# Router products in four column groups, more zero products in waits, and four reorderings of a two-block transformer kernel

## The reference

```
first_block:                                   # weights read once, 384 MB of them in the experts
  mod = silu(c) @ w_ada + b_ada                # six vectors: shifts, scales, gates
  h = rms_norm(x)*(1+sc1)+sh1 ; y = mixer(h)   # sliding attention + gated linear attention, @ w_out
  x = x + gt1*rms_norm(y, g_post_mix)
  h = rms_norm(x)*(1+sc2)+sh2
  logits = h @ w_router + b_router             # 256 x 32; the top 4 of 32 experts for each row
  y = sum over chosen e of gate_e * expert_e(h)   # expert: (u @ w1 + b1), limited swiglu, @ w2 + b2
  x = x + gt2*rms_norm(y, g_post_ffn)
second_block:
  h += 0.5*swiglu(rmsnorm(h), gate, up, down)              # 1024 -> 2816 -> 1024
  z = rmsnorm(h) @ w_in
  attn = moba_attention(q, k, v)                           # from z
  gm = u * (W_s @ layernorm(v) + b_s)                      # chunked spatial gating, from gelu(z)
  h += (sigmoid gates * (attn @ w_a, gm @ w_g)) @ w_out
  h += 0.5*swiglu(...) ; return rmsnorm(h, final_norm)
```

## Time and profile before

| what | us |
|---|---|
| median of 3 runs | 1649.52 |
| lowest, highest | 1648.58, 1654.21 |
| the profiled execution | 1654.21 |
| its span, first to last instruction | 1652.5 |
| PE busy in the span | 1459.1 (88%) |
| mean granted clock of TensorE | 0.94 of full |

### The profile page before, as it was taken

The page is one execution under the profiler, slowest core; times in us unless marked ns, Lnnn a source line. Parts: engine busy times, 40 slices in busy tenths (PEclk is TensorE's granted clock), DMA queues, the critical chain, the costliest instruction groups (busy, mean ns, idle before and its releaser), DMA issues.

```text
span 1652.5 us, 20611 instructions
## 1 busy us (share of the span) xinstructions
PE 1459.1 (88%) x8409; PEld 844.1 (51%) x8414; DVE 589.2 (36%) x957; ACT 471.5 (29%) x836; POOL 123.5 (7%) x254
## 2 busy tenths in 40 slices
PE   5999987896868787897687888899999999999998
PEld 3768433342322232332232333248888878788886
DVE  3675212220110111221110211146654677666654
ACT  3544201110110110111000101046553674565643
POOL 2001301110110110110110110000000010000000
PEclk9998999997888897999898998899999999999999
DMA  9998999999999999999999999976555433555440
GB/s 383 410 359 348 372 424 426 425 424 426 425 425 424 427 423 425 423 386 427 425 422 423 425 424 425 408 311 225 185 183 199 179 129 126 214 206 195 178 162 26
DMA packets 76953, 547.45 MB, mean 331 GB/s; under 512 B 8660, under 2 KB 9044, under 8 KB 11112
## 3 DMA queue, kind: packets, MB, share of 16 engines
q1 hardware_dynamic: 75744, 542.95, 80.6%
q10 hardware_dynamic: 1032, 2.16, 0.4%
HBM read 544.03 MB, written 1.06 MB: 330 GB/s over the span
## 4 chain that ended last, share of the span: by engine, by line
PE 65%; DMA 25%; issue 4%; DVE 3%; POOL 1%; ACT 1%; PEldq 1%; SPq 0%; POOLq 0%; DVEq 0%; ACTq 0%
PE bank L309 62%; DMA slot<-w_mlp 24%; PE bank L313 2%; DMA slot<-w_in_tail 1%; PEldq L85 1%; SPq L336 0%; DVE u_l L327 0%; DVE u_g L323 0%; DVE u_l L324 0%; DVE u_s L319 0%; PE bank L1451 0%; POOL oh L324 0%; POOL ow L324 0%; DVE h L327 0%; DVE XL L319 0%
## 5 line engine op out<-in xcount | busy, mean ns | idle before, releaser
L309 PE MATMUL bank<-slot,xt 128*32 128x512 f32 (+1 forms) x2048 | 377.7, 682 | 71.6 <-DMA slot<-w_mlp 70.7
L309 PEld LDWEIGHTS bank<-slot,xt 128*32 128x32 f32 (+1 forms) x2048 | 95.2, 129 | 345.6 <-issue 178.7
L309 PE MATMUL bank<-wht,XH 128*128 128x512 f32 x528 | 207.5, 397 | 4.4 <-DVE wlt L319 2.7
L327 DVE SCALAR_TENSOR_TENSOR wlt<-slot,colt,wht 128x512 fp32r<-128x512 f32 x248 | 177.3, 760 | 79.1 <-ACT wht L316 78.8
L323 DVE TENSOR_SCALAR u_g<-bank 64x512 f32<-64x512 f32 (+1 forms) x34 | 23.3, 686 | 510.8 <-PE bank L309 503.5
L309 PE MATMUL bank<-wht,XL 128*128 128x512 f32 x528 | 204.0, 391 | 0.0
L309 PE MATMUL bank<-wlt,XH 128*128 128x512 f32 x528 | 203.9, 391 | 0.0
L316 ACT ACTIVATE wht<-slot,colt 128x512 fp32r<-128x512 f32 x248 | 164.4, 718 | 92.3 <-PE bank L309 92.2
L316 ACT ACTIVATE u_s<-u_g 64x512 f32<-64x512 f32 (+1 forms) x34 | 21.4, 630 | 533.0 <-DVE u_g L323 533.0
L309 PE MATMUL bank<-slot,at 128*32 128x256 f32 (+1 forms) x1664 | 160.3, 431 | 6.8 <-DMA slot<-w_mlp 3.6
L309 PEld LDWEIGHTS bank<-slot,at 128*32 128x32 f32 (+1 forms) x1664 | 65.9, 116 | 95.6 <-issue 65.5
(11 more groups left out here) (321 smaller groups left out, 1485.5 us busy)
## 6 DMA issues: line engine op xcount, KB each, us to landing
slot<-w_mlp SPq DMA_DIRECT2D x384, 1024.0 KB, 27.0
slot<-gu SPq DMA_DIRECT2D x44, 1024.0 KB, 4.8
slot<-w_ada SPq DMA_DIRECT2D x24, 1024.0 KB, 10.0
slot<-down SPq DMA_DIRECT2D x22, 1024.0 KB, 4.8
slot<-w_in SPq DMA_DIRECT2D x18, 1024.0 KB, 5.3
slot<-w_out SPq DMA_DIRECT2D x8, 1024.0 KB, 8.4
slot<-w_gate SPq DMA_DIRECT2D x8, 1024.0 KB, 4.8
slot<-w_br_a SPq DMA_DIRECT2D x2, 1024.0 KB, 5.2
```

What stands on the lines that cost most here:

```text
L309: return pe(lambda e: e.matmul(o, l, r, start=start, stop=stop), *after, **kw)
L327: return dve(lambda e: e.scalar_tensor_tensor(o, a, s, b, op0, op1), *after)
```

## The change

- In the wait for the first weights (L620 to L627): 5 more zero products.
- residual gets later: with it, both gained products and the two sums in h are emitted by the returned function. Only the second half of the last residual ahead of the tail uses it.
- logits: four products side by side in the four column groups (weights wrt of 32 columns, 128 moving columns of h2t), two sets of four for each half; ScalarE copies the 128x128 sum to at, and one product with the new constant sum4 adds the four groups. The transposes of half 1 are emitted in two fours, with zero products between; rows_out moves behind the second logits_out on ScalarE's queue. From the router to the gather there are now 19 zero products instead of 7, on bank 6 instead of bank 4.
- swiglu: u_l goes ahead of the product u_s.
- layer_norm moves from the last span of w_in2 to the third span of gates, spatial_gate from the first span of gates to the fourth.
- first_merged splits one piece more before its transposes.

```diff
@@ -225,6 +225,7 @@
         stat0, stat1 = (keep(n, [128, 32]) for n in ("stat0", "stat1"))
         brs = keep("brs", [128, NE])
         zero = keep("zero", [128, 64])
+        sum4 = keep("sum4", [128, NE])
         near = keep.at
         z0 = near + NEAR * SLOT
         slots = [
@@ -460,6 +461,7 @@
             )
         )
         t_zs = tt(pool, zsel[:, :], ident[:, 0:64], ident[:, 64:128], ALU.add, t_id)
+        t_sum4 = tt(pool, sum4[:, :], zsel[:, 0:NE], zsel[:, NE : 2 * NE], ALU.add, t_zs)
 
 
         c_t, gpre_mix, gpre_ffn, gn1, gnm, gn2 = (colt[:, 8 * i : 8 * i + 8] for i in range(6))
@@ -620,10 +622,11 @@
         x_t(0)
         first_products([4])
         t_xt = x_t(1)
+        warm(1, 6)
         first_products([5])
-        warm(3, 6)
+        warm(5, 6)
         first_products([6])
-        warm(3, 6)
+        warm(5, 6)
         t_mod = first_products([7])
         warm(3, 6)
         t_mod = tt(dve, mod[:, :], bank[0][:, :], bias_ada[0][:, :], ALU.add, t_mod, t_ada)
@@ -1103,7 +1106,7 @@
                     pieces[first + k]["used"] = t
             return toks
 
-        def residual(b, t, y_of, gg, t_gg, col, tmp, sqr):
+        def residual(b, t, y_of, gg, t_gg, col, tmp, sqr, later=False):
 
 
             at_ = lambda i: stat[:, col + 4 * b + i : col + 4 * b + i + 1]
@@ -1117,15 +1120,24 @@
 
 
             t1 = square(0, t[0], act.now())
-            free[y_of[b][0]] = [gained(0, t1)]
-            t1 = square(1, t[1])
-            t_r = rsqrt_sum(at_(3), at_(0), at_(1), t1)
-            free[y_of[b][1]] = [gained(1, t1)]
-            t2 = dve.now()
-            return lambda: [
-                stt(h[:, b, c], tmp[:, b, c], at_(3), h[:, b, c], ALU.mult, ALU.add, t_r, t2)
-                for c in (slice(0, 512), slice(512, 1024))
-            ]
+            t2 = square(1, t[1])
+            if not later:
+                free[y_of[b][0]] = [gained(0, t1)]
+            t_r = rsqrt_sum(at_(3), at_(0), at_(1), t2)
+
+            def finish():
+                if later:
+                    free[y_of[b][0]] = [gained(0, t1)]
+                    free[y_of[b][1]] = [gained(1, t2)]
+                t = dve.now()
+                return [
+                    stt(h[:, b, c], tmp[:, b, c], at_(3), h[:, b, c], ALU.mult, ALU.add, t_r, t)
+                    for c in (slice(0, 512), slice(512, 1024))
+                ]
+
+            if not later:
+                free[y_of[b][1]] = [gained(1, t2)]
+            return finish
 
         y_of = ((0, 1), (4, 5))
         mixh, mixl = (lambda k, a=a, g=g: a[:, k, :] if k < 4 else g[:, k, :] for a, g in ((atth1, XH), (attl1, XL)))
@@ -1175,9 +1187,10 @@
         t_tr, t_ns = [[], []], []
         nscale = [stat[:, 26 + 2 * b : 27 + 2 * b] for b in range(2)]
 
-        def columns_of(b):
+        def columns_of(b, gs):
             toks = []
-            for g, bk in enumerate((2, 3)):
+            for g in gs:
+                bk = 2 + g
                 for j in range(4):
                     k = 4 * g + j
                     t = tr(bank[bk][:, 128 * j : 128 * j + 128], h[:, b, k * 128 : k * 128 + 128], t_h[b][g], *free[bk],
@@ -1188,11 +1201,17 @@
         def columns_out(q, b, g, t):
             t_tr[b].append(evac(q, h2t[:, 4 * g : 4 * g + 4, b * 128 : b * 128 + 128], 2 + g, t[g], src=three))
 
-        def logits(b, bk):
-            for k in range(8):
-                t = mm(bank[bk][:, 0:NE], h2t[:, k, b * 128 : b * 128 + 128], wrt[:, k, :], k == 0, k == 7,
-                       t_tr[b][k // 4], T["wrt"], *free[bk], sig=k == 7)
+        def logits(b, g):
+
+            for q in range(4):
+                k = 4 * g + q
+                t = mm(bank[b][32 * q : 32 * q + 32, 0:128], wrt[:, k, :], h2t[:, k, b * 128 : b * 128 + 128], g == 0, g == 1,
+                       t_tr[b][g], T["wrt"], *free[b], sig=g == 1 and q == 3)
             return t
+
+        def logits_out(b, t):
+            t = af(at[:, b, :], bank[b][:, 0:128], ACT.Copy, t)
+            return mm(bank[b][:, 0:NE], at[:, b, :], sum4[:, :], True, True, t, t_sum4, sig=True)
 
 
         def chosen(b, bk, t):
@@ -1241,43 +1260,55 @@
 
         def add_nothing(n):
             for _ in range(n):
-                mm(bank[4][:, :], zero[:, :].bitcast(BF16), moving_zero, False, False)
+                mm(bank[6][:, :], zero[:, :].bitcast(BF16), moving_zero, False, False)
 
         for g in range(2):
             t_sq = squares(sqr, 0, halves[g], 29 + g, t_h[0][g])
         t_ns.append(rsqrt_sum(nscale[0], stat[:, 29:30], stat[:, 30:31], t_sq))
         rest.append(residual(1, t[1], y_of, gg, T["gg"], 16, tmp2, sqr))
-        t = columns_of(0)
+        t = columns_of(0, (0, 1))
         columns_out(act, 0, 0, t)
         columns_out(act, 0, 1, t)
         start_sums((6, 7))
         t_h.append(rest[1]())
         for i in (9, 10, 11):
             slot_gate[NEAR + i].append(t_h)
-        t_l0 = logits(0, 0)
-        t = columns_of(1)
+        logits(0, 0)
+        add_nothing(1)
+        t_l0 = logits(0, 1)
+        add_nothing(1)
+        t_l0 = logits_out(0, t_l0)
+        t = columns_of(1, [0])
+        add_nothing(1)
+        t += columns_of(1, [1])
         for g in range(2):
             t_sq = squares(sq2, 1, halves[g], 31 + g, t_h[1][g])
         columns_out(dve, 1, 0, t)
         columns_out(act, 1, 1, t)
+        add_nothing(1)
+        logits(1, 0)
+        add_nothing(2)
+        t_l1 = logits(1, 1)
+        add_nothing(2)
+        t_ns.append(rsqrt_sum(nscale[1], stat[:, 31:32], stat[:, 32:33], t_sq))
+        t_l1 = logits_out(1, t_l1)
         T["gg2"] = rows_out(2, s_gg2, T["gr"])
-        t_ns.append(rsqrt_sum(nscale[1], stat[:, 31:32], stat[:, 32:33], t_sq))
         selections(0)
-        t_l1 = logits(1, 1)
         t_ypz = fill(pool, ypair[:, :], 0.0, t_l1)
 
         t_sl0 = chosen(0, 0, t_l0)
         t_sl1 = chosen(1, 1, t_l1)
         start_sums((4, 5))
         t_p0 = mm(bank[0][:, 0:NE], tri_s[:, :], sel[:, 0, :], True, True, t_sl0, t_tris, *free[0], sig=True)
+        add_nothing(1)
         mm(bank[1][:, 0:NE], ones[:, :], sel[:, 0, :], True, False, t_ones, *free[1])
-        add_nothing(2)
+        add_nothing(4)
         t_p1 = mm(bank[1][:, 0:NE], tri_s[:, :], sel[:, 1, :], False, True, t_sl1, sig=True)
         placed(0, 0, t_p0)
         placed(1, 1, t_p1)
         mm(bank[0][:, 0:NE], ones[:, :], sel[:, 0, :], True, False, *free[0])
         t_cn = mm(bank[0][:, 0:NE], ones[:, :], sel[:, 1, :], False, True, sig=True)
-        add_nothing(1)
+        add_nothing(2)
         t_first = [[one_hot(dve, oh, 0, s_, b) for b in range(2)] for s_ in range(2)]
         slot_gate[NEAR + 8] += [T["gg2"], T["brs"]]
         t_cnt = cp(dve, cnt[:, :], bank[0][0:1, 0:NE], t_cn)
@@ -1345,9 +1376,9 @@
             t_g_ = ts(dve, u_g[:, :], bank[X][:, :], 7.0, ALU.min, t_x, *after)
             free[X] = [t_g_]
             t_s_ = af(u_s[:, :], u_g[:, :], ACT.Sigmoid, t_g_, scale=1.702)
-            t = tt(dve, u_s[:, :], u_g[:, :], u_s[:, :], ALU.mult, t_s_)
             t_l_ = ts(dve, u_l[:, :], bank[Y][:, :], 7.0, ALU.min, t_y, *after, s2=-7.0, op1=ALU.max)
             free[Y] = [t_l_]
+            t = tt(dve, u_s[:, :], u_g[:, :], u_s[:, :], ALU.mult, t_s_)
             return stt(u_l[:, :], u_l[:, :], 1.0, u_s[:, :], ALU.add, ALU.mult, t, t_l_)
 
         def transposed(X, dst, t_a):
@@ -1741,7 +1772,7 @@
         p_gu1 = add_pieces(c_gu1, gains=gn1)
         split_to(p_gu1)
         t_h = [residual(0, t[0], acc, gg2, T["gg2"], 16, tmp3, sqr)(), None]
-        rest = residual(1, t[1], acc, gg2, T["gg2"], 16, tmp3, sqr)
+        rest = residual(1, t[1], acc, gg2, T["gg2"], 16, tmp3, sqr, later=True)
 
         def rest_1():
             t_h[1] = rest()
@@ -1966,7 +1997,7 @@
         t_zu = [scaled(act, zu[:, b, :], b, b, t[b], ACT.Gelu_apprx_tanh) for b in range(2)]
         t = span(p_in_2 + 12, 4, 512, 6, XH2, XL2, x2_of, {1: scores2_1})
         t_zg = [scaled(act, zg[:, b, :], 6 + b, b, t[b], ACT.Gelu_apprx_tanh) for b in range(2)]
-        t = span(p_in_2 + 16, 4, 512, 0, XH2, XL2, x2_of, {0: scores2_0, 1: layer_norm, 2: inputs_t})
+        t = span(p_in_2 + 16, 4, 512, 0, XH2, XL2, x2_of, {0: scores2_0, 2: inputs_t})
         t_zv = [scaled((act, dve)[b], zv[:, b, :], b, b, t[b]) for b in range(2)]
 
         def gates(i, b0, hooks):
@@ -2030,10 +2061,10 @@
                     T["gm"].append([th, tl])
 
         t_g = [[] for _ in range(4)]
-        gates(0, 6, {0: softmax2_1, 2: spatial_gate})
+        gates(0, 6, {0: softmax2_1})
         gates(1, 0, {0: turned2_1, 2: values2_1})
-        gates(2, 6, {0: turned2_0, 2: values2_0})
-        gates(3, 0, {})
+        gates(2, 6, {0: turned2_0, 1: layer_norm, 2: values2_0})
+        gates(3, 0, {2: spatial_gate})
         ya, yg = ((2, 3), (4, 5)), ((6, 7), (0, 1))
         t = rows(p_bra, 4, ktile(atth), ktile(attl), lambda k, b: [T["v1"], T["v0"]], ya,
```

(2 more changed lines are left out.)

## The result

The changed kernel takes 1662.04 us (median of 5; 1661.18 to 1662.68) against 1649.52 (median of 5; 1648.58 to 1654.21). The ratio is 1.0071 with a 95% interval of 1.0055 to 1.0088: slower by 12.5 us between the medians, where 9.0 faster was forecast. The profiled execution of the changed kernel took 1662.32, with a span of 1660.5. Lines lie one number or more higher than before (L309 is now L310).

A forecast was written before the change was run, and what follows sets the result against it. The DMA stream was taken to bound the expert part, its gap in the router the part ahead, TensorE the tail; 4.8 + 0.6 - 1.05 + 1.05 + 3.6 = 9.0 off the median 1649.52 gave 1640.5 us, range 1637 to 1647.5.

The forecast's parts named there:

- Router, the path: Second half's router products to the gather: shorter products gain about 1.3 us, zero products take it back; net nothing.
- rival 4: Clock falls earlier, before 153, in the router; slower than before, 1650.2 or 1651.9 us; chance 0.05.
- Router, the clock: Clock stays up through gather, bias products and expert 0's first group, so the next chunk goes earlier; 4.8 us saved.
- rival 2: The median already had the clock up in the router, so that term is nearly 0; 1645.3 us; chance 0.20.
- the sum: All terms together, 9.0 us gained, taken against the median: 1640.5 us; chance 0.44.
- rows_out: Row copy about 1 us later on ScalarE's queue; the 19th chunk goes at about 159.6, costing nothing below 161.
- Last swiglu: Last expert: u_l fills VectorE's wait for the sigmoid, 0.6 us gained; in the other experts hidden by the stream.
- Start of the tail: Tail's first steps: tmp products now stand ahead of the third weight piece, so TensorE comes later; a loss of 1.05 us.
- layer_norm: Moved to the third gate span: TensorE's wait at the old place goes, 1.05 us gained; nothing counted at the new place.
- Rival 3: VectorE's slowing moves along with layer_norm and TensorE waits at the new place; 1642.5 us; chance 0.08.
- Merge: w_out2's second piece split earlier, so the third piece's products start at 1436.5 instead of 1440.13; 3.6 us gained.
- Start: Five more zero products lie in waits for the first weights; nothing gained or lost, 0.3 us lost at most.

The follow-up runs named there:

- e1: The whole change, but with the new tile sum4 in the last 128 bytes of memory so the slots keep their old addresses; 1649.51 us, +0.4 against the kernel before.
- e3: The kernel before with only an unused tile of 256 bytes a partition ahead of the slots; 1648.79 us, -0.4 against the kernel before.
- e10: The kernel before with one line changed, the split of one more piece ahead of the merge; 1644.91 us, -3.8 against the kernel before.
- e5: The kernel before with the router's part and zero products alone, sum4 in the last 128 bytes; 1650.05 us, +2.0 against the kernel before.
- e7: e1 with rows_out moved back ahead of the second half's router products; 1647.69 us, -0.3 against the kernel before.
- e13: The kernel before with the merge's split and the swiglu's new order in all experts; 1647.25 us, -1.1 against the kernel before.
- e17: e14 with the swiglu's new order in the last expert alone; 1643.23 us, -5.6 against the kernel before.
- e14: The kernel before with the merge's split and the layer norm's new place; 1643.29 us, -5.1 against the kernel before.
- e16: The kernel before with the merge's split and the tail's first steps in their new order; 1646.28 us, -2.1 against the kernel before.
- e6: The kernel before with all of the change but the router's part and zero products; 1646.96 us, -1.0 against the kernel before.
- e8: e6 with the tail's first steps in their old order; 1646.19 us, -1.8 against the kernel before.
- e18: e14 with the new zero products at the start and between the old router products; 1644.02 us, -4.8 against the kernel before.

## Why the prediction was wrong, step by step

- **The term that was missing.** "Router, the path" counts the sum product with sum4 as work of TensorE and never as bytes ahead of the slots: their address was put at nothing without a reason. The experiments put the cost there. Cost: 12 of the 12.5 us (the change at +12.5, e1 at +0.4). No rival had it: rival 4, the slow side, was looked for in the clock, which held.
- **Router, the clock** (-4.8). In the profiled execution the mechanism and the size were right: first group to second gather and the pieces ahead of it came out as worked out: the second gather is 4.2 us earlier, 5.5 counted from the router's transposes (5.2 worked out). But it was taken off a median that didn't contain the low clock. This is rival 2, at 0.20; the prediction named the 4.7 us between the runs as just the size of the term and still gave the sum twice the chance. Against the median it is worth 0: in e3 and e10, at the median, the router ran at 1.00 with the old products.
- **Router, the path** (0) and rows_out (0). Together +2.0 (e5): 0.4 later at the gather, the row copy's transfer 0.9 later, worth about 0.7 by the medians (e7). That transfer went at 161.00, just where the text set the limit of "harmless". In the changed kernel that is 11.1 behind its transposes. The rest of the 2.0 isn't split up.
- **Last swiglu** (-0.6). Right in place: u_g to the tail's first product took 19.34 in e13 and in e17 against 19.94 in e10; the 0.5 between e17 and e14 is less than the intervals. Wrong in "in the other experts it is hidden by the stream": with the order in them too, the kernel loses 2.7. After the address and the clock this is the largest miss.
- **Start of the tail** (+1.05). 1.8 between e16 and e10, 0.8 between e6 and e8; locally 9.08 against 8.00 from h to the first long product. Three of e16's 12 runs lie 5 us above its median; without such runs on either side its difference is 1.1. Right in size. The wait itself is put down to ScalarE's XH (0.76), which follows from the later h; the weight piece that the prediction named ends at the same time (1120.2), so which of the two binds isn't told.
- **layer_norm** (-1.05, with nothing for the new place). -1.2 (e14 against e10), near the limit of what the medians can tell; in the traces, behind the last u_g, 564.8 us against 566.2. Right. The four operations take 6.13 on GpSimd at the new place, and the weight piece beside them takes 3.48 on VectorE, so the slowing did move along, but TensorE doesn't wait. Rival 3 didn't come.
- **Merge** (-3.6). -3.8 alone, and 566.2 against 569.9 behind the last u_g (e10 against e3). Right. **Start** (0): in e18 not more than 0.3, with the router's zeros.
- **The balance.** -3.8 - 1.2 + 2.7 + 0.8 to 1.8 is -1.5 to -0.5; e6 has -1.0. With the router +2.0, 0.5 to 1.5; e1 has +0.4. With the slots 12.1, 12.5. Against the 9.0 of the sum, e1 is 9.4 short: 4.8 are the clock, 2.0 the router's path, 3.3 the swiglu (-0.6 forecast, +2.7 measured); the other terms moved by less than 1.

The best version found is e17: merge, layer norm, and the swiglu's order in the last expert alone, 1643.23 us, 5.6 less in the median than the kernel before beside it (ratio over all runs 0.9975, since 3 of its 12 runs lie 5 to 7 us above the median). With the 12.5 that makes some 18 less than the changed kernel. It doesn't beat e14 by more than the measurement can tell.

## What to carry to other kernels

A new tile is also an address: ask what lies behind it, and keep the buffers that a full-rate stream writes on multiples of 256 bytes, since 128 bytes of scratch cost more here than all the reorderings together could earn. A gain read from one profiled execution counts against a median only if that execution is like the median; when the profiled one is the highest, what it shows may be just what sets it apart. And an order inside a shared helper is to be costed at each of its callers, with the wait that stands there and with the code that it adds.

## What the runs showed of the hardware

- A stream of 8 KB rows into the on-chip memory ran at 425 GB/s with destinations on multiples of 256 bytes, 419 at 64 and 128 bytes past one, 417 at 32 and 224 past one (309, 312 and 313 ns for a row, in the median). The share of the DMA engines' time read as full in each case.
- A piece of 8 KB of code more, fetched at 20.6 to 22.4 us, goes with a weight chunk of 1 MB that lands 3.2 to 3.4 us behind the one before it, in place of 2.4 to 2.5 (7 profiles against 13). That the one causes the other isn't shown.
- The same program ran the router at 1.00 of the clock in some executions and at 0.50 in others. In the two profiles of the latter the clock fell at 156 to 157, ahead of the gather, and came back at about 170. With the new router, whose waits hold more zero products, no run in 40 had a time like these (in e18, with the zero products alone, none in 6), against 8 in 127 of the kernel before.
